# Two transformer blocks at sequence 256: other places in SBUF for the weight buffers, the 256-column activations and the chunks of the gated hidden layer

## Chip, cores and metric

The kernel runs on one core of one Trainium2 chip. The metric is the device time of one execution in microseconds. The engines are named as in the profile: PE (TensorE matmuls), PEld (its weight loads), DVE (VectorE), ACT (ScalarE), POOL (GpSimd), SP (SyncE).

## What is computed

Two transformer blocks in fp32, one after the other, on 256 positions of width 2048 (`D`). The first puts 16 meta tokens ahead (272 positions, `T`), and runs neighbourhood attention, latent attention and a gated MLP with a short convolution. The second is conditioned on a vector `c` and runs a gated convolution, a gated linear recurrence over 8 heads, two output gates and a second gated MLP. Cut to the products with large weights:

```python
# first block, h: 272 x 2048
proj = rmsnorm(h) @ w_in                          # 2048 x 3904
q, kv = rmsnorm(cq) @ w_q_up, rmsnorm(ckv) @ w_kv_up
h = h + concat(rmsnorm(out_a), rmsnorm(out_b)) @ w_out
hn = rmsnorm(h)
h = h + (silu(conv3(hn @ w_gate)) * (hn @ w_up)) @ w_down      # D_FF = 5632
# second block, x: 256 x 2048
mod = silu(c) @ w_ada + b_ada                     # scales, shifts and gates
proj = (rmsnorm(x) * (1 + sc_m) + sh_m) @ w_in_2  # 2048 x 11264
merged = sigmoid(gate_a) * (conv_part @ w_conv_out) + sigmoid(gate_b) * (hgrn_part @ w_hgrn_out)
x = x + gt_m * (merged @ w_o)
h2 = rmsnorm(x) * (1 + sc_f) + sh_f
x = x + gt_f * ((silu(h2 @ w_ffn_gate) * (h2 @ w_ffn_up)) @ w_ffn_down)
return rmsnorm(x)
```

## The kernel before

**Layout.** Activations are kept transposed: 128 features on the partitions, positions along the free axis. A chunk is 128 features by 256 (or 272, or 258) positions. `D` is 16 chunks (`KD`), half of `D_FF` is 22 (`HALF`).

**Split products.** A product in fp32 precision is made of three in fp32r. Each weight and each activation is split in a hi part and a lo part (what is left), and hi times hi, hi times lo and lo times hi are added up in PSUM. Weights come by DMA in slabs of 2048 columns of 4 bytes (`raw`, three buffers); ACT copies the hi part to `wh` (line 1301), DVE subtracts and writes the lo part to `wl` (line 1811); both have three buffers `wh0..wh2`, `wl0..wl2`, of 8192 bytes a partition each. An activation tile has a first axis of 2, hi plane and lo plane: `xx` (272 columns a chunk), `xs`, `hid`, `conv`, `oo` (256 columns a chunk).

**The gemm.** The host part lays out all products as slabs and gemms in one order (`make_plan`), and every engine's program walks the same order, tied together by semaphores. In `gemm` (lines 704 to 706) a slab of 256 output columns has 8 chunks of weights; for each chunk k and each of two column tiles j of 128 there are three matmuls:

- line 704: weights `wh`, moving operand the hi plane of chunk k
- line 705: weights `wh` again, moving operand the lo plane of chunk k
- line 706: weights `wl`, moving operand the hi plane of chunk k

So a chunk is six matmuls, and each has its own weight load. `gemm_raw` (lines 671 to 673) does the same on activations that aren't scaled yet, `gemm_by_head` (lines 732 to 734) for the latent attention. Attention, the recurrence and the conditioning vector run as generators ("lanes") that are pumped between the chunks of the gemms.

**Places.** What the change touches is the place of an operand, its byte address within a partition modulo 256 (`ROW_BYTES`). `row_home(offset, place)` gives the next address at a wanted place. `wh` starts at place 128. All slabs, chunks and column tiles of weights are multiples of 256 bytes apart, so all weights in `wh` are read from place 128. Between `wh` and `wl` lie `rstd` and two tiles `ssq`, so `wl` is at 128 + 192 = 64 (mod 256). `xx` follows `wl`, at place 64. Its chunks are 1088 bytes long, each 64 further on than the one before. A gemm that reads columns 16 to 271 (the up gemms of the first gated block, 256 columns) so reads chunk k from place 128 + 64k, one that reads columns 14 to 271 (its gate gemms, 258 columns) from 120 + 64k. `xs`, `hid`, `conv` and `oo` have chunks of 1024 bytes, and are placed at `wh_off + 64`: every chunk in both planes is read from place 192.

**The gated hidden layer.** `hid` holds 22 chunks, hi and lo. For each unit ACT writes the hi part (line 1660) and DVE the lo part (line 2257), and the eight down gemms of each half read them all: 32 down gemms in the kernel, of 22 chunks. While a gated block begins, its input (`raw_ffn`, `raw_mix`) lies in the same memory, before `hid` is written.

Of the kernel before, what the change touches and what calls it, by code (L numbers as in the profile page):

```python
# [7 lines left out]
F32 = mybir.dt.float32  # L8
# [5 lines left out]
P = 128  # L14
# [12 lines left out]
GRID = 64  # L27
SLAB = 2048
ROW_BYTES = 256

ORDER = "q0 m0 k0 v0 q1 m1 k1 v1 m2 q2 k2 v2 m3 q3 k3 v3".split()

# [273 lines left out]
def build(nc, A, out):  # L306
    ctx = ExitStack()
    with ctx:
# [9 lines left out]
        def sb(name, shape, dt=F32):  # L318
            t, cursor[0] = at(name, shape, dt, cursor[0])
            cursor[0] = (cursor[0] + 31) // 32 * 32  # L320
            return t
# [7 lines left out]
        raw = [sb(f"raw{i}", [P, SLAB]) for i in range(NR)]  # L329
        wh_off = cursor[0]  # L330
        wh = [sb(f"wh{i}", [P, SLAB], F32R) for i in range(NS)]
        rstd = sb("rstd", [P, T])
        ssq = {n: sb(f"ssq_{n}", [P, T]) for n in "ha"}
        assert (cursor[0] - wh_off) % ROW_BYTES == 192
        wl = [sb(f"wl{i}", [P, SLAB], F32R) for i in range(NS)]
        xoff = cursor[0]
        xx = sb("xx", [P, 2, KD, T], F32R)
        xs, _ = at("xs", [P, 2, KD + 1, SEQ], F32R, row_home(xoff, wh_off + 64))
        hoff = cursor[0]
        H = sb("H", [P, KD, T])  # L340
        cst = sb("cst", [P, NCONST])
# [5 lines left out]
        nx_off = cursor[0]  # L347
        nx = [sb(f"nx{i}", [P, T]) for i in range(NXB)]
        sqt = [sb(f"sqt{i}", [P, T]) for i in range(2)]
        ssq["b"] = sb("ssq_b", [P, T])  # L350
        ada_off = cursor[0]
        ada_raw = [sb(f"ada_raw{i}", [P, 512]) for i in range(NADA)]
        ada_acc = sb("ada_acc", [P, 512])
# [36 lines left out]
        assert off <= mla_end  # L390

        raw_in, _ = at("raw_in", [P, 2, KD, T], F32R, limit // 32 * 32 - 8 * KD * T)
        ffn_home = row_home(arena, wh_off + 64)
        raw_ffn = [at(f"raw_ffn{i}", [P, 2, 8, T], F32R, ffn_home + (2 + 22 * i) * SEQ * 4)[0] for i in range(2)]
        raw_mix, _ = at("raw_mix", [P, 2, 6, T - Q0], F32R, ffn_home + 2 * HALF * SEQ * 4)
        cursor[0] = ffn_home
        hid = sb("hid", [P, 2, HALF, SEQ], F32R)
        gct = [sb(f"gc{i}", [P, SEQ]) for i in range(NGC)]

        cursor[0] = mix_home = row_home(arena, wh_off + 64)  # L400
        conv = sb("conv", [P, 2, 8, SEQ], F32R)
        cursor[0] = oo_home = row_home(cursor[0], wh_off + 64)
        oo = sb("oo", [P, 2, 8, SEQ], F32R)
        cu = sb("cu", [P, 2, SEQ])
        cy = sb("cy", [P, 2, SEQ])
# [14 lines left out]
        cu2 = sb("cu2", [P, 2, SEQ])  # L420
        cy2 = sb("cy2", [P, 2, SEQ])

        OPERAND = {X0: xx, XS: xs, XQ: cqx, XKV: ckvx, XB: xb, XHID: hid, XOC: conv, XOH: oo}
        NORM_DST = [xx, cqx, ckvx, xb, xx, xx]
        NORM_T0 = [0, Q0, 0, Q0, Q0, Q0, 16, 16]
        NORM_D = [D, 512, 256, 1024, 1024, D, D, D]
# [212 lines left out]
        def tensor_program(pe):  # L639
# [40 lines left out]

            def gemm(key, ready=None):
                g = GEMMS[key]
                x = OPERAND[g.operand]
                n = g.t1 - g.t0
                for j, b in enumerate(g.banks):
                    if g.use[j] > 1:
                        pe.wait_ge(s_bank[b], g.use[j] - 1)
                for i in g.slabs:
                    _, _, k0, nk, _, ncols = SLABS[i]
                    last = i == g.slabs[-1]  # L690
                    h = wh[i % NS][:, 0:nk * ncols].rearrange("p (c n) -> p c n", c=nk)
                    l = wl[i % NS][:, 0:nk * ncols].rearrange("p (c n) -> p c n", c=nk)
                    for c in range(nk):
                        k = k0 + c
                        if c == 0:
                            pe.wait_ge(s_lo, 2 * i + 1)
                        if c == nk // 2:
                            pe.wait_ge(s_lo, 2 * i + 2)
                        if ready is not None:
                            ready(k)  # L700
                        end = last and c == nk - 1
                        for j, (o, w) in enumerate(g.tiles):
                            dst = ps[g.banks[j]][0:w, 0:n]
                            pe.matmul(dst, h[:, c, o:o + w], x[:, 0, k, g.t0:g.t1], start=(k == 0), stop=False)  # L704
                            pe.matmul(dst, h[:, c, o:o + w], x[:, 1, k, g.t0:g.t1], start=False, stop=False)  # L705
                            m = pe.matmul(dst, l[:, c, o:o + w], x[:, 0, k, g.t0:g.t1], start=False, stop=end)  # L706
                            if c == nk - 1 and j == len(g.tiles) - 1:
                                m.then_inc(s_slab, 1)
                        if c in ticks(nk):
                            lanes.pump(c == nk - 1 or c == nk // 2 - 1)  # L710
# [577 lines left out]
        def scalar_program(act):  # L1288
# [326 lines left out]
            def ffn(b):  # L1615
                gc_use = 2 * HALF * (b - 1)
                for f in range(2):
                    for g in range(HALF // 2):
                        gate, up = (b, "gate", f, g), (b, "up", f, g)
                        first_use = gc_use + HALF * f + 2 * g  # L1620

                        def silu():
                            yield
                            for j in range(2):
                                if f == 0 and g < 2:
                                    act.wait_ge(s_ft, 2 * g + j + 1)
                                else:
                                    act.wait_ge(*last_use(gate, j))
                                gc = gct[(first_use + j) % NGC]
                                act.activation(gc[:, :], gc[:, :], ACT.Silu).then_inc(s_silu, 1)  # L1630

                        gemm(gate)
                        act.wait_ge(s_slab, done(gate))
                        for j in range(2):
                            u = first_use + j
                            gc, src = gct[u % NGC], ps[j]
                            if u - gc_use >= NGC or b == 2:
                                act.wait_ge(s_hidl, u - NGC + 1)
                            n = HALF * f + 2 * g + j
                            if f == 0 and g < 2:  # L1640
                                act.wait_ge(*last_use(gate, j))
                            if b == 1:
                                if f == 0 and g < 2:
                                    src = ssq["ab"[j]]
                                act.activation(gc[:, :], src[:, 2:258], ACT.Identity, bias=V("cb", n), scale=V("cw1", n)).then_inc(s_gca, 1)
                            elif f == 0 and g < 2:
                                act.activation(gc[:, :], gc[:, :], ACT.Silu, bias=shift_of(4 * g + j)).then_inc(s_fu, 1)
                            else:
                                s, _ = last_use(gate, j)
                                act.activation(gc[:, :], src[:, 0:256], ACT.Silu).then_inc(s, 1)  # L1650
                        if b == 1:
                            lanes.start("silu", silu(), slow=True, front=True)
                        gemm(up)
                        lanes.drain("silu")
                        for j in range(2):
                            u = first_use + j
                            act.wait_ge(*last_use(up, j))
                            if f == 1 and g == 0 and j == 0:
                                act.wait_ge(s_slab, done((b, "down", 0, 7)))
                            act.activation(hid[:, 0, 2 * g + j, :], gct[u % NGC][:, :], ACT.Copy).then_inc(s_hidh, 1)  # L1660
                    for g in range(8):
                        gemm((b, "down", f, g))
                        for j in range(2):
                            if f == 1:
                                c = 2 * g + j
                                squares(N_MIX2 if b == 1 else 8, c, H[:, c, 16:T], *last_use((b, "down", 1, g), j))
                        if b == 1 and f == 1:
                            if g == 1:
                                act.wait_ge(s_gain, 2)
                                raw_shift_hi(N_MIX2)  # L1670
                            raw_his(N_MIX2, RAW_LAG[N_MIX2].get(g, []))
                        if b == 2 and f == 1 and g:
                            final_gain(2 * g - 2)
                            final_gain(2 * g - 1)
                        if f == 1 and g == 0:
                            ready_sqrt()
# [123 lines left out]
        def vector_program(dve):  # L1800
# [392 lines left out]
            def ffn(b):  # L2193
                gc_use = 2 * HALF * (b - 1)
                for f in range(2):
                    for g in range(HALF // 2):
# [37 lines left out]
                        for j in range(2):  # L2234
# [19 lines left out]
                            else:  # L2254
                                dve.tensor_tensor(gc[:, :], ps[2 + j][:, 0:256], gc[:, :], ALU.mult).then_inc(s, 1)
                            dve.wait_ge(s_hidh, u + 1)
                            dve.tensor_tensor(hid[:, 1, 2 * g + j, :], gc[:, :], hid[:, 0, 2 * g + j, :].bitcast(F32), ALU.subtract).then_inc(s_hidl, 1)
                    if b == 2 and f == 0:
                        mod_until(24)
                    for g in range(8):  # L2260
# [278 lines left out]
```

## Time and profile before

| | |
|---|---|
| median of 3 runs | 2701.86 us (2701.0 to 2703.86) |
| the profiled execution's own time | 2700.86 us |
| its span, first to last instruction | 2699.5 us |
| granted clock of TensorE, mean | 0.995 |
| PE busy | 2645.3 us, 98% |
| DVE, ACT, POOL busy | 68%, 46%, 12% |
| matmuls | 22052 |
| of them with 256 columns at a constant place (xs, hid, conv, oo, in `gemm`) | 3 x 4544 = 13632 |

Matmuls overlap, so the busy time of one (some 280 ns) is longer than the distance from its start to the start of the next. That distance is read from the timeline, as the start of one matmul subtracted from the start of a later one, divided by the number between them.

### The profile page before, as it was taken

The numbers are of one execution on the slowest core, as the hardware profiler recorded it, in microseconds if no ns is written. First come the engines' busy times: TensorE is split into PE (matmuls) and PEld (weight loads), VectorE is DVE, ScalarE is ACT, GpSimd is POOL, SyncE is SP. The second block draws the span as 40 slices with busy tenths as digits, with TensorE's granted clock in tenths as the row PEclk, the third lists the DMA queues.
The fourth block names the chain that finished last, engine by engine and source line by source line (L and its number), as shares of the span: only waits on it lengthen the run. The fifth ranks groups of instructions, "written<-read, shape, count | busy, mean of one in ns | idle before, by whom it ended". The sixth has DMA issues, their size and how long they took to land.

```text
span 2699.5 us, 51384 instructions
## 1 busy us (share of the span) xinstructions
PE 2645.3 (98%) x22052; PEld 2606.7 (97%) x22052; DVE 1844.0 (68%) x2592; ACT 1248.4 (46%) x1943; POOL 331.5 (12%) x526
## 2 busy tenths in 40 slices
PE   7999999999999999999999999999999999999998
PEld 7888889999999999999999999999999999999998
DVE  6666568877777777787888667776877644444444
ACT  5556655544433444445444443334554443444443
POOL 2110101111121111231000001110211000000001
PEclk9999999999999999999999999999999999999999
DMA  6433345678788887886444568886768656555553
GB/s 204 137 106 103 118 148 173 205 267 269 263 293 278 277 270 262 272 285 207 152 147 155 188 225 279 273 279 217 256 208 273 219 192 191 195 188 190 187 186 126
DMA packets 500084, 571.22 MB, mean 212 GB/s; under 512 B 26704, under 2 KB 473424, under 8 KB 499856
## 3 DMA queue, kind: packets, MB, share of 16 engines
q1 hardware_dynamic: 467968, 463.76, 52.6%
q0 software_dynamic: 31600, 103.80, 11.9%
q8 instruction: 174, 2.85, 0.4%
q10 hardware_dynamic: 288, 0.36, 0.1%
q14 instruction: 54, 0.44, 0.0%
HBM read 565.77 MB, written 2.54 MB: 211 GB/s over the span
## 4 chain that ended last, share of the span: by engine, by line
PE 86%; DVE 7%; ACT 4%; issue 1%; DMA 1%; POOL 0%; SPq 0%; DVEq 0%; ACTq 0%
PE ps L704 27%; PE ps L705 27%; PE ps L706 26%; DVE wl L1811 3%; ACT wh L1301 2%; PE ps L1002 1%; PE ps L833 1%; DMA raw<-in_w_in 1%; DVE nx L1915 1%; DVE lr L2007 1%; ACT lp L1476 0%; PE ps L806 0%; PE ps L858 0%; PE ps L859 0%; PE ps L671 0%
## 5 line engine op out<-in xcount | busy, mean ns | idle before, releaser
L1811 DVE TENSOR_TENSOR wl<-raw,wh 128x1024 fp32r<-128x1024 f32 (+1 forms) x894 | 1058.9, 1200 | 577.0 <-ACT wh L1301 572.7
L1301 ACT ACTIVATE wh<-raw 128x1024 fp32r<-128x1024 f32 (+1 forms) x894 | 883.2, 1030 | 606.1 <-PE ps L706 587.8
L704 PE MATMUL ps<-xs,wh 128*128 128x256 f32 x2880 | 811.3, 282 | 5.8 <-DVE xs L1892 5.8
L705 PE MATMUL ps<-xs,wh 128*128 128x256 f32 x2880 | 799.4, 278 | 0.0
L706 PE MATMUL ps<-xs,wl 128*128 128x256 f32 x2880 | 796.7, 277 | 0.0
L704 PEld LDWEIGHTS ps<-xs,wh 128*128 128x128 f32 x2880 | 539.9, 187 | 7.6 <-DVE wl L1811 5.8
L705 PEld LDWEIGHTS ps<-xs,wh 128*128 128x128 f32 x2880 | 545.0, 189 | 1.0 <-issue 1.0
L706 PEld LDWEIGHTS ps<-xs,wl 128*128 128x128 f32 x2880 | 539.5, 187 | 0.0
L704 PE MATMUL ps<-xx,wh 128*128 128x258 f32 (+3 forms) x1840 | 530.2, 288 | 3.7 <-DVE xx L1894 3.7
L705 PE MATMUL ps<-xx,wh 128*128 128x258 f32 (+3 forms) x1840 | 522.3, 284 | 0.0
L706 PE MATMUL ps<-xx,wl 128*128 128x258 f32 (+3 forms) x1840 | 522.3, 284 | 0.0
L704 PE MATMUL ps<-hid,wh 128*128 128x256 f32 x1408 | 393.4, 279 | 0.0
L705 PE MATMUL ps<-hid,wh 128*128 128x256 f32 x1408 | 390.1, 277 | 0.0
L706 PE MATMUL ps<-hid,wl 128*128 128x256 f32 x1408 | 388.8, 276 | 0.0
L704 PEld LDWEIGHTS ps<-xx,wh 128*128 128x128 f32 (+1 forms) x1840 | 347.9, 189 | 8.8 <-DVE wl L1811 3.7
L1162 POOL DMA_DIRECT2D ada_raw<-in_w_ada x384 | 206.7, 538 | 1193.4 <-DVE ada_acc L2060 1055.7
L705 PEld LDWEIGHTS ps<-xx,wh 128*128 128x128 f32 (+1 forms) x1840 | 348.3, 189 | 0.7
L706 PEld LDWEIGHTS ps<-xx,wl 128*128 128x128 f32 (+1 forms) x1840 | 347.5, 189 | 0.0
L2060 DVE SCALAR_TENSOR_TENSOR ada_acc<-ada_raw,small,ada_acc 128x512 f32<-128x512 f32 x360 | 268.4, 746 | 0.0
L705 PEld LDWEIGHTS ps<-hid,wh 128*128 128x128 f32 x1408 | 266.2, 189 | 0.0
L704 PEld LDWEIGHTS ps<-hid,wh 128*128 128x128 f32 x1408 | 263.4, 187 | 0.0
L706 PEld LDWEIGHTS ps<-hid,wl 128*128 128x128 f32 x1408 | 263.3, 187 | 0.0
(378 smaller groups left out, 2753.2 us busy)
## 6 DMA issues: line engine op xcount, KB each, us to landing
raw<-in_w_in SPq DMA_DIRECT2D x118, 1024.0 KB, 5.3
ada_raw<-in_w_ada POOLq DMA_DIRECT2D x384, 256.0 KB, 4.8
raw<-in_w_gate SPq DMA_DIRECT2D x44, 1024.0 KB, 6.5
raw<-in_w_up SPq DMA_DIRECT2D x44, 1024.0 KB, 7.1
raw<-in_w_ffn_gate SPq DMA_DIRECT2D x44, 1024.0 KB, 5.2
raw<-in_w_ffn_up SPq DMA_DIRECT2D x44, 1024.0 KB, 5.3
raw<-in_w_down SPq DMA_DIRECT2D x32, 1024.0 KB, 6.0
raw<-in_w_ffn_down SPq DMA_DIRECT2D x32, 1024.0 KB, 5.4
```

What stands on the lines that cost most here:

```text
L704: pe.matmul(dst, h[:, c, o:o + w], x[:, 0, k, g.t0:g.t1], start=(k == 0), stop=False)
L705: pe.matmul(dst, h[:, c, o:o + w], x[:, 1, k, g.t0:g.t1], start=False, stop=False)
L706: m = pe.matmul(dst, l[:, c, o:o + w], x[:, 0, k, g.t0:g.t1], start=False, stop=end)
L833: m = pe.matmul(bank[0:w, 0:keys_of(j)], l[:, o:o + w], r[:, 0:keys_of(j)], start=(i == 0), stop=(i == len(qk) - 1))
L1002: m = pe.matmul(bank[:, 128 * j:128 * j + 128], k[:, n, 128 * b:128 * b + 128], q[:, n, 128 * b:128 * b + 128], start=True, stop=True)
L1162: pool.dma_start(ada_raw[i % NADA][:, :], w[:, k, 512 * g:512 * g + 512]).then_inc(s_ada[i % NADA], 16)
L1301: act.activation(wh[i % NS][:, part], raw[i % NR][:, part], ACT.Copy).then_inc(s_hi, 1)
L1811: dve.tensor_tensor(wl[i % NS][:, part], raw[i % NR][:, part], wh[i % NS][:, part].bitcast(F32), ALU.subtract).then_inc(s_lo, 1)
L1915: dve.scalar_tensor_tensor(out=x, in0=norm_src(n, i), scalar=norm_gain(n, i), in1=rstd[:, 0:m], op0=ALU.mult, op1=ALU.mult).then_inc(s_nx, 1)
L2007: dve.reciprocal(r[:, :], r[:, :]).then_inc(s_ldve[lane], 1)
L2060: dve.scalar_tensor_tensor(out=ada_acc[:, :], in0=r, scalar=s, in1=ada_acc[:, :], op0=ALU.mult, op1=ALU.add).then_inc(s_acc, 1)
```

## The change

All weights go to place 128 (`rstd` and `ssq` move behind, to the small tiles), `xs`, `hid`, `conv` and `oo` go from place 192 to place 64, and `xx` starts at place 128 in place of 64. In `hid` the chunks are no longer all at one place: after every fourth chunk there is a gap of 8 columns (32 bytes), so chunks 0 to 3 are at place 64, 4 to 7 at 96, 8 to 11 at 128, 12 to 15 at 160, 16 to 19 at 192, 20 and 21 at 224. A plane of `hid` gets 64 columns more, so that the lo plane has the same places. The number, order, shapes and waits of all instructions stay.

```diff
+HID_STEP = 8
+HID_PLANE = HALF * 256 + 64
...
         wh = [sb(f"wh{i}", [P, SLAB], F32R) for i in range(NS)]
-        rstd = sb("rstd", [P, T])
-        ssq = {n: sb(f"ssq_{n}", [P, T]) for n in "ha"}
-        assert (cursor[0] - wh_off) % ROW_BYTES == 192
+        assert (cursor[0] - wh_off) % ROW_BYTES == 0
         wl = [sb(f"wl{i}", [P, SLAB], F32R) for i in range(NS)]
         xoff = cursor[0]
         xx = sb("xx", [P, 2, KD, T], F32R)
-        xs, _ = at("xs", [P, 2, KD + 1, SEQ], F32R, row_home(xoff, wh_off + 64))
+        xs, _ = at("xs", [P, 2, KD + 1, SEQ], F32R, row_home(xoff, wh_off - 64))
...
-        ssq["b"] = sb("ssq_b", [P, T])
+        rstd = sb("rstd", [P, T])
+        ssq = {n: sb(f"ssq_{n}", [P, T]) for n in "hab"}
...
-        ffn_home = row_home(arena, wh_off + 64)
-        raw_ffn = [at(f"raw_ffn{i}", [P, 2, 8, T], F32R, ffn_home + (2 + 22 * i) * SEQ * 4)[0] for i in range(2)]
-        raw_mix, _ = at("raw_mix", [P, 2, 6, T - Q0], F32R, ffn_home + 2 * HALF * SEQ * 4)
+        ffn_home = row_home(arena, wh_off - 64)
+        raw_ffn = [at(f"raw_ffn{i}", [P, 2, 8, T], F32R, ffn_home + (2 * SEQ + i * HID_PLANE) * 4)[0] for i in range(2)]
+        raw_mix, _ = at("raw_mix", [P, 2, 6, T - Q0], F32R, ffn_home + 2 * HID_PLANE * 4)
         cursor[0] = ffn_home
-        hid = sb("hid", [P, 2, HALF, SEQ], F32R)
+        hid = sb("hid", [P, 2, HID_PLANE], F32R)
...
-        cursor[0] = mix_home = row_home(arena, wh_off + 64)
+        cursor[0] = mix_home = row_home(arena, wh_off - 64)
         conv = sb("conv", [P, 2, 8, SEQ], F32R)
-        cursor[0] = oo_home = row_home(cursor[0], wh_off + 64)
+        cursor[0] = oo_home = row_home(cursor[0], wh_off - 64)
         oo = sb("oo", [P, 2, 8, SEQ], F32R)
...
+        def hidden_at(h, c):
+            return hid[:, h, c * SEQ + c // 4 * HID_STEP:(c + 1) * SEQ + c // 4 * HID_STEP]
+
+        def moving(g, h, k):
+            return hidden_at(h, k) if g.operand == XHID else OPERAND[g.operand][:, h, k, g.t0:g.t1]
...
-                            pe.matmul(dst, h[:, c, o:o + w], x[:, 0, k, g.t0:g.t1], start=(k == 0), stop=False)
-                            pe.matmul(dst, h[:, c, o:o + w], x[:, 1, k, g.t0:g.t1], start=False, stop=False)
-                            m = pe.matmul(dst, l[:, c, o:o + w], x[:, 0, k, g.t0:g.t1], start=False, stop=end)
+                            pe.matmul(dst, h[:, c, o:o + w], moving(g, 0, k), start=(k == 0), stop=False)
+                            pe.matmul(dst, h[:, c, o:o + w], moving(g, 1, k), start=False, stop=False)
+                            m = pe.matmul(dst, l[:, c, o:o + w], moving(g, 0, k), start=False, stop=end)
...
-                            act.activation(hid[:, 0, 2 * g + j, :], gct[u % NGC][:, :], ACT.Copy).then_inc(s_hidh, 1)
+                            act.activation(hidden_at(0, 2 * g + j), gct[u % NGC][:, :], ACT.Copy).then_inc(s_hidh, 1)
...
-                            dve.tensor_tensor(hid[:, 1, 2 * g + j, :], gc[:, :], hid[:, 0, 2 * g + j, :].bitcast(F32), ALU.subtract).then_inc(s_hidl, 1)
+                            dve.tensor_tensor(hidden_at(1, 2 * g + j), gc[:, :], hidden_at(0, 2 * g + j).bitcast(F32), ALU.subtract).then_inc(s_hidl, 1)
```

## Rows read from the trace of the kernel before

**Rows 1.** The page: busy time of each engine, and the granted clock in 40 slices.
```profile
PE 2645.3 (98%) x22052; PEld 2606.7 (97%) x22052; DVE 1844.0 (68%) x2592; ACT 1248.4 (46%) x1943; POOL 331.5 (12%) x526
...
PEclk9999999999999999999999999999999999999999
```

**Rows 2.** The waits of PE: total us, times, longest us.
```profile
PE ps L671 <- DVE wl L1811: 15.0, 2, 14.1
```

**Rows 3.** Groups by line and shape: busy us, mean ns | idle us before.
```profile
L704 PE MATMUL ps<-xs,wh 128*128 128x256 f32 x2880 | 811.3, 282 | 5.8 <-DVE xs L1892 5.8
L705 PE MATMUL ps<-xs,wh 128*128 128x256 f32 x2880 | 799.4, 278 | 0.0
L706 PE MATMUL ps<-xs,wl 128*128 128x256 f32 x2880 | 796.7, 277 | 0.0
L704 PE MATMUL ps<-hid,wh 128*128 128x256 f32 x1408 | 393.4, 279 | 0.0
L705 PE MATMUL ps<-hid,wh 128*128 128x256 f32 x1408 | 390.1, 277 | 0.0
L706 PE MATMUL ps<-hid,wl 128*128 128x256 f32 x1408 | 388.8, 276 | 0.0
...
L704 PE MATMUL ps<-xx,wh 128*128 128x256 f32 x672 | 189.1, 281 | 3.5 <-DVE xx L1894 3.5
L705 PE MATMUL ps<-xx,wh 128*128 128x256 f32 x672 | 188.7, 281 | 0.0
L706 PE MATMUL ps<-xx,wl 128*128 128x256 f32 x672 | 188.5, 281 | 0.0
...
L2257 DVE TENSOR_TENSOR hid<-gc,hid 128x256 fp32r<-128x256 f32 x88 | 37.5, 426 | 42.7 <-ACT hid L1660 42.7
...
L704 PE MATMUL ps<-conv,wh 128*128 128x256 f32 x128 | 35.8, 280 | 0.0
L704 PE MATMUL ps<-oo,wh 128*128 128x256 f32 x128 | 35.7, 279 | 0.0
```

**Rows 4.** Timeline of PE (start us, us): first chunks of gemms of hid and xs, last ones.
```profile
2243.32 0.28 PE L704 MATMUL ps<-hid,wh 128*128 128x256 f32 x1
...
2246.09 0.28 PE L704 MATMUL ps<-hid,wh 128*128 128x256 f32 x1
...
2257.88 0.28 PE L704 MATMUL ps<-hid,wh 128*128 128x256 f32 x1
...
1686.64 0.28 PE L704 MATMUL ps<-xs,wh 128*128 128x256 f32 x1
...
1691.49 0.28 PE L704 MATMUL ps<-xs,wh 128*128 128x256 f32 x1
```

**Rows 5.** Timeline of PE: starts of chunks 0, 4 to 8 and 15, an up gemm.
```profile
529.65 0.28 PE L704 MATMUL ps<-xx,wh 128*128 128x256 f32 x1
...
532.46 0.28 PE L704 MATMUL ps<-xx,wh 128*128 128x256 f32 x1
...
533.17 0.28 PE L704 MATMUL ps<-xx,wh 128*128 128x256 f32 x1
...
533.89 0.28 PE L704 MATMUL ps<-xx,wh 128*128 128x256 f32 x1
...
534.60 0.28 PE L704 MATMUL ps<-xx,wh 128*128 128x256 f32 x1
...
535.30 0.28 PE L704 MATMUL ps<-xx,wh 128*128 128x256 f32 x1
...
540.27 0.28 PE L704 MATMUL ps<-xx,wh 128*128 128x256 f32 x1
```

**Rows 6.** Timeline of PEld: the load that starts with the matmul at 2246.09.
```profile
2246.10 0.19 PEld L705 LDWEIGHTS ps<-hid,wh 128*128 128x128 f32 x1
```

**Rows 7.** Timeline of PE: starts of chunks 0 and 15, a gate gemm.
```profile
587.07 0.28 PE L704 MATMUL ps<-xx,wh 128*128 128x258 f32 x1
...
597.86 0.28 PE L704 MATMUL ps<-xx,wh 128*128 128x258 f32 x1
```

More of the change, by code:

```diff
@@ L421, in build @@
         cy2 = sb("cy2", [P, 2, SEQ])
-        OPERAND = {X0: xx, XS: xs, XQ: cqx, XKV: ckvx, XB: xb, XHID: hid, XOC: conv, XOH: oo}
+        OPERAND = {X0: xx, XS: xs, XQ: cqx, XKV: ckvx, XB: xb, XOC: conv, XOH: oo}
+        def hidden_at(h, c):
+            return hid[:, h, c * SEQ + c // 4 * HID_STEP:(c + 1) * SEQ + c // 4 * HID_STEP]
+        def moving(g, h, k):
+            return hidden_at(h, k) if g.operand == XHID else OPERAND[g.operand][:, h, k, g.t0:g.t1]
         NORM_DST = [xx, cqx, ckvx, xb, xx, xx]
@@ L682, in gemm @@
                 g = GEMMS[key]
-                x = OPERAND[g.operand]
                 n = g.t1 - g.t0
```

## Prediction

> **What bounds the kernel now.** I read the page first, then the waits of the matmul engine, then its groups by line and shape, and last the start times of single matmuls. The page [rows 1] has PE busy in 2645.3 of 2699.5 us, DVE in 68% and ACT in 46% of it, and a granted clock of 9 tenths or more in every slice (0.995 in the mean, that is the 2.4 GHz level). So the kernel is as long as its stream of 22052 matmuls. The waits confirm it: the longest entry is 15.0 us in the first gemm [rows 2], the next is 5.8 us, ahead of line 704 on xs [rows 3], and what follows is smaller still. Nothing that feeds PE is late often enough to matter, and a DVE or ACT instruction that became some per cent faster or slower would not be seen. What is left to change is the cadence, the time from the start of one matmul to the start of the next.
>
> **How long one is busy is not the cadence.** The groups [rows 3] show 277 to 282 ns for a matmul of 256 columns, but these overlap. The starts tell more. In a down gemm of the second gated block [rows 4] line 704 starts its first chunk at 2243.32 and its last at 2257.88: 21 chunks of six matmuls in 14.56 us, 693.3 ns a chunk, 115.6 ns a matmul. In a gemm of `xs` it is 7 chunks in 4.85 us, 693 ns. In an up gemm of the first block [rows 5], same columns, same weight buffers, same clock, it is 15 chunks from 529.65 to 540.27, 708 ns a chunk, 118.0 ns a matmul. The only thing that sets them apart is where the moving operand lies. `hid` and `xs` have all chunks 1024 bytes apart, so all at place 192 of 256. `xx` has chunks of 272 columns, 1088 bytes, so each lies 64 bytes further on, and its chunk k is read from place (128 + 64k) mod 256. Inside this gemm the chunks differ too [rows 5]: chunk 4 (place 128) takes 532.46 to 533.17, 0.71 us; chunk 5 (place 192) 0.72; chunk 6 (place 0) 0.71; chunk 7 (place 64) 0.70. So placement does act on the cadence, by a few ns a matmul, and two things count: whether the place stays, and which place it is. In the weight loads of that down gemm [rows 4, 6] one sees why they could be linked: the load for the next matmul starts at 2246.10, when the present matmul starts (2246.09), so each matmul's first columns are read together with the next one's weights.
>
> **Part 1, constant-place tiles other than hid.** What I follow is the difference "place of the columns minus place of the weights that are loaded meanwhile". During lines 704, 705 and 706 those weights are in wh, wl and wh. Before, with wh at 128, wl at 64 and columns at 192, the difference is 64, 128, 64. After, with both at 128 and columns at 64, it is 192, 192, 192. The trace has no steady stream at 192, so I bound it from both sides. Nearest rows: the chunks of [rows 5]. The chunk at place 192 has differences (64, 128, 64) and takes 0.72 us; the one at place 64 has (192, 0, 192) and takes 0.70, the shortest of the four; place 0 with (128, 192, 128) and place 128 with (0, 64, 0) lie between. At the rows' 10 ns that is some 17 to 20 ns in six, about 2.8 ns a matmul in favour of 192. The steady stream, though, has already shed 27 ns of the 720 that the same differences cost in `xx`, and part of that may be the same loss. I take half, 1.4 ns. It holds for xs, conv and oo: 3 x (2880 + 128 + 128) = 9408 matmuls [rows 3], so 9408 x 1.4 ns = -13 us. The fast end is the whole 2.8 ns, -26 us.
>
> The slow end comes from [rows 3]. Among the three matmuls of a unit, line 704 is the one behind which the next load goes to the same buffer and place (wh after wh), and it is busy longest: 279 ns in `hid` against 277 and 276 for 705 and 706. If the equal place of successive weights is the cause of that, after the change all three are such: 3 x 279 against 279 + 277 + 276 is 5 ns a unit, 1.7 ns a matmul, +16 us on these 9408.
>
> **Part 2, hid.** The 22 chunks of a down gemm no longer lie at one place: four at 64, four at 96, then 128, 160, 192, and two at 224. That is 4224 matmuls in 32 gemms. Three terms. (a) Steps: in [rows 5], where the place steps at every chunk, a chunk takes 708 ns against 693 without; 15 ns a step, 5 steps a gemm, 32 gemms: +2.4 us. (b) Places that are no multiple of 64 (96, 160, 224: 10 of 22 chunks). The nearest row is a gate gemm [rows 7], read from column 14, so at places 120 + 64k and with 258 columns: 15 chunks from 587.07 to 597.86, 719 ns. Two more columns at 2.4 GHz are 0.8 ns a matmul, 5 a chunk, so 6 ns a chunk are left over 708, 1 ns a matmul, on 10/22 x 4224 = 1920 matmuls: +1.9 us. (c) The differences pass over all of (64, 128, 64)'s alternatives, whose mean chunk, 708, is 12 ns shorter than the 720 at place 192; half again, 1 ns a matmul: -4.2 us. Sum 0. Bounds: if hid falls to the mixed cadence of `xx` throughout, 118.0 instead of 115.6, 4224 x 2.4 ns = +10 us; at best (c) counts whole and the others nothing, -8 us.
>
> **Part 3, xx and the other tiles of 272 columns.** Their places move on by 64 at every chunk before and after, and over four chunks each of the three loads meets all four differences in either layout. Lines 704, 705 and 706 are busy 281 ns each in the 256-column form of `xx` [rows 3], so here the move of wl has no price by line: 0. The bound is half a ns either way on the 3 x 1840 matmuls of `xx`, 3 us.
>
> **Part 4, the rest.** `rstd` and `ssq` move to another address, the hi copy (line 1660) and the low half (line 2257) write 32 bytes further on; none gains an instruction or a wait, no DMA is added, and the order on every queue stays. The cover is PE: DVE is idle a third of the time, ACT more than half [rows 1]. 0. If this cover were gone, 88 writes of 426 ns [rows 3] would be 37 us in all, and a per cent of them is nothing.
>
> **Sum.** -13 + 0 + 0 + 0 = -13 us. The profiled execution took 2700.86 us around its span of 2699.5, so 2688; the median of the runs shown is 1 us above it, 2701.86, so 2689.
>
> **A page beside it.** The rows show that matmuls with the same columns cost 115.6 or 118.0 ns by place [rows 4, 5]. The Trainium skill, TensorE: Matmul & The Clock Gate, "Step-by-step: what each phase is for", says that TensorE reads its moving operand and its next weights through two independent ports, so that a load takes nothing from a running matmul. By that rule no placement matters and the sum would be 0. The trace disagrees. The same page, "Back-to-back issue gap", has N/2.4 + 2.5 ns from start to start, 109.2 ns at 256 columns, an estimate by which placement could give back at most 6.4 ns on each of 13632 matmuls, 87 us; no row here comes near it.
>
> **The rivals.**
>
> *Slower: equal places of successive weights cost.* It is the slow end of part 1, in hid as well: 13632 x 1.7 ns = +23 us, 2724 us. For it speaks that line 704 is busiest in every constant-place tile (279, 277, 276 in hid; 282, 278, 277 in xs; 280 and 279 for line 704 in conv and oo) [rows 3]. Against it: in `xx` the same line has the same wh-after-wh and shows nothing (281, 281, 281). It decides as soon as it costs over 1.4 ns, the gain of part 1.
>
> *No change in xs: only constancy counts.* The 27 ns between the chunk at place 192 in `xx` and the steady chunk are more than all that separates the four places. If a stream at any one place settles into the same 693 ns, part 1 is 0. In hid only (a) and (b) are left, +4 us: 2706 us, at the edge of what can be told from no change. For it: xs, hid, conv and oo have one cadence at different distances between their hi and lo halves. Against it: these all have the same differences, so they can't tell.
>
> *Hid loses its steadiness.* Part 1 is 0 and hid pays the mixed cadence, +10 us: 2712. For it: the up gemms never settle, over 15 chunks [rows 5]. Against it: they step every six matmuls, hid every 24.
>
> *Placement does nothing*, by the rule of two ports: 2702. In the form that the trace allows, the differences in `xx` come from its row length, and not from where it stands towards the weights. It has little for it, as chunks 4 to 7 have one length and differ.
>
> **How the numbers follow.** Forecast 0.46; slower by equal weights 0.20; only constancy 0.16; hid loses 0.12; nothing 0.06. The forecast's own range runs from -26 - 8 + 3 (2671) to about 2698. The range for 8 in 10 goes up to 2724, where the slow case stands, and down to 2673. A measurement of this kernel tells about 0.2%, 5.4 us, from no change. The forecast case is faster but for a tenth of it, with a little from the others: faster 0.45. Half of "only constancy", all of "nothing" and that tenth: same 0.20. The rest: slower 0.35.
>
> **What would show it.** Right: in the starts of line 704, seven chunks of `xs` in 4.80 us instead of 4.85 (685 ns each), lines 704, 705 and 706 equally busy in xs, conv and oo; 21 chunks of hid in 14.5 to 14.6 us; an up gemm's 15 chunks still in 10.6 us. Slower case: busy 279 or more on all three lines and 7 chunks in 4.92 us. Only constancy: 4.85 again, though with another split over the three lines. Hid's own case: 21 chunks in about 14.8 us. The prediction is wrong in its ground if `xs` moves by more than 3 ns a matmul either way: then a steady stream has states that the stepping stream of `xx` doesn't show.

## The result and the profile after

The changed kernel takes 2716.3 us in the median (2712.4 to 2719.0, 4 runs), the kernel before 2702.1 us in the same comparison: ratio 1.0047, 95% interval 1.0032 to 1.0062. So it is slower by 0.5%, where a faster kernel, 2689 us, had been forecast. The profiled execution took 2717.0 us. The four runs lie 6.6 us apart, those of before 2.9.

The page of the kernel after, for [rows 1]:

```profile
span 2715.6 us, 51384 instructions
...
PE 2660.4 (98%) x22052; PEld 2620.8 (97%) x22052; DVE 1844.6 (68%) x2592; ACT 1248.8 (46%) x1943; POOL 330.9 (12%) x526
```

Same instructions, same clock (0.994 against 0.995); PE is busy 15.1 us longer, and the span is 16.1 us longer. The waits of PE are as before, the largest again the first slab's, 15.8 us. The whole difference is cadence. The groups by line and shape after, for [rows 3]; the edit moved lines 704 to 706 to 710 to 712:

```profile
L710 PE MATMUL ps<-xs,wh 128*128 128x256 f32 x2880 | 811.3, 282 | 5.8 <-DVE xs L1898 5.8
L711 PE MATMUL ps<-xs,wh 128*128 128x256 f32 x2880 | 804.6, 279 | 0.0
L712 PE MATMUL ps<-xs,wl 128*128 128x256 f32 x2880 | 804.5, 279 | 0.0
L710 PE MATMUL ps<-hid,wh 128*128 128x256 f32 x1408 | 396.3, 281 | 0.0
L712 PE MATMUL ps<-hid,wl 128*128 128x256 f32 x1408 | 395.3, 281 | 0.0
L711 PE MATMUL ps<-hid,wh 128*128 128x256 f32 x1408 | 394.9, 280 | 0.0
...
L712 PE MATMUL ps<-xx,wl 128*128 128x256 f32 x672 | 187.4, 279 | 0.0
```

The three lines are now nearly alike, and hid has gone from 279, 277, 276 to 281, 280, 281. (The 282 of line 710 on xs contains 68 longer matmuls, 0.39 us in the mean, most of them behind matmuls of a lane; without them it is 279, before and after.) The starts show more. The timeline of PE in the same down gemm of hid, for [rows 4], at chunks 0, 4, 8, 12, 16, 20 and 21:

```profile
2249.79 0.28 PE L710 MATMUL ps<-hid,wh 128*128 128x256 f32 x1
...
2252.62 0.28 PE L710 MATMUL ps<-hid,wh 128*128 128x256 f32 x1
...
2255.46 0.28 PE L710 MATMUL ps<-hid,wh 128*128 128x256 f32 x1
...
2258.33 0.28 PE L710 MATMUL ps<-hid,wh 128*128 128x256 f32 x1
...
2261.16 0.28 PE L710 MATMUL ps<-hid,wh 128*128 128x256 f32 x1
...
2263.99 0.28 PE L710 MATMUL ps<-hid,wh 128*128 128x256 f32 x1
...
2264.70 0.28 PE L710 MATMUL ps<-hid,wh 128*128 128x256 f32 x1
```

21 chunks in 14.91 us against 14.56: 710 ns for the six matmuls of a chunk against 693. By fours the chunks take 2.83, 2.84, 2.87, 2.83 and 2.83 us, and the dearest, 8 to 11, are those at place 128, where the weights are too. And two stretches of xs, each from chunk 0 to chunk 7 of a gemm:

```profile
1659.90 0.28 PE L710 MATMUL ps<-xs,wh 128*128 128x256 f32 x1
...
1664.66 0.28 PE L710 MATMUL ps<-xs,wh 128*128 128x256 f32 x1
...
1737.99 0.28 PE L710 MATMUL ps<-xs,wh 128*128 128x256 f32 x1
...
1742.94 0.28 PE L710 MATMUL ps<-xs,wh 128*128 128x256 f32 x1
```

The first takes 4.76 us, 680 ns a chunk; the second 4.95 us, 707 ns. Same code, same places, same clock: there are two cadences. The kernel before has two as well, which the rows shown so far don't tell: nearly all of its stream at constant places runs at 693, but one stretch of xs doesn't. Its timeline there, ahead of four transposes of a lane (L806) and behind them:

```profile
1995.22 0.28 PE L704 MATMUL ps<-xs,wh 128*128 128x256 f32 x1
...
2025.61 0.28 PE L704 MATMUL ps<-xs,wh 128*128 128x256 f32 x1
...
2027.02 0.60 PE L806 MATMUL ps<-cst,ada_acc 128*128 128x128 f32 x4
...
2028.52 0.28 PE L704 MATMUL ps<-xs,wh 128*128 128x256 f32 x1
...
2035.46 0.28 PE L704 MATMUL ps<-xs,wh 128*128 128x256 f32 x1
```

Ahead of the transposes 43 chunks take 30.39 us, 706.7 ns each; behind them ten take 6.94, 694 each. With the 7.5 us before 1989.1 that is some 40 us of the kernel before at 707.

After the change the stream holds each cadence over long stretches; in the last gate and up gemms it stays in the slow one for 240 us. The stretch view of the kernel after there (length, then PE busy and, in brackets, the number of matmuls):

```profile
2328.00:2570.00 242.00, 242.00 (x2057) 242.00 (x2056) 118.54 (x128) 99.65 (x128) 0.00 (x0) 1.00 0.58 186
```

and of the kernel before in the same gemms:

```profile
2320.00:2560.00 240.00, 240.00 (x2079) 240.00 (x2079) 118.86 (x129) 101.34 (x130) 0.00 (x0) 1.00 0.58 190
```

242 us for 2057 matmuls is 117.6 ns each, 240 for 2079 is 115.4. After the change every chunk in this stretch takes 706 or 707 ns, though DVE is busy in half of it only and ACT in two fifths. In an up gemm of the first block, 15 chunks now run from 533.16 to 543.68, 10.52 us, where [rows 5] have 10.62.

Over all matmuls that follow each other directly, from the timeline's starts: hid went from 115.6 to 118.3 ns (+11.5 us in all), xs from 115.8 to 116.1 (+2.8), the 256-column form of `xx` from 118.0 to 117.0 (-2.0), the rest by less than half a us each. That is 11.3 of 16.1 us; 4.1 of the others lie where lane matmuls and waits interrupt the stream, about 2 of them in the attention, and 0.6 ahead of the first matmul.

### The profile page after: what moved, and what is told of

Read it like the earlier page. It is cut to its first block, busy times and chain, and to the rows that moved or that the text cites. A ratio compares the mean times of both kernels' runs of the same rounds, so it can differ in the third digit from the quotient of the medians.

```text
span 2715.6 us, 51384 instructions
## 1 busy us (share of the span) xinstructions
PE 2660.4 (98%) x22052; PEld 2620.8 (97%) x22052; DVE 1844.6 (68%) x2592; ACT 1248.8 (46%) x1943; POOL 330.9 (12%) x526
## 4 chain that ended last, share of the span: by engine, by line
PE 87%; DVE 7%; ACT 4%; issue 1%; DMA 0%; POOL 0%; SPq 0%; DVEq 0%; ACTq 0%
PE ps L710 27%; PE ps L711 26%; PE ps L712 26%; DVE wl L1817 3%; ACT wh L1307 1%; PE ps L1008 1%; PE ps L839 1%; PE ps L678 1%; PE ps L680 1%; PE ps L679 1%; DVE nx L1921 1%; DVE lr L2013 1%; DMA raw<-in_w_in 0%; PE ps L855 0%; PE ps L865 0%
## 5 line engine op out<-in xcount | busy, mean ns | idle before, releaser
L712 PE MATMUL ps<-hid,wl 128*128 128x256 f32 x1408 | 395.3, 281 | 0.0
```

Source lines behind the costliest of these rows:

```text
L712: m = pe.matmul(dst, l[:, c, o:o + w], moving(g, 0, k), start=False, stop=end)
```

## The experiments

The two theories as I held them after this profile: **(T)** what counts is the difference "place of the columns minus place of the weights loaded meanwhile"; a stream at a constant place falls into a cadence of its own for each set of differences, sometimes one of two. **(E)** Equal places of successive weights cost, the slower rival of the prediction. Below, "(a, b)" is the difference, modulo 256, when the weights loaded meanwhile are of wh, then when they are of wl: before is (64, 128), after is (192, 192). "Chunk" is the six matmuls of a chunk at a constant place, between interruptions; its ns come from the one execution that was traced. Each ratio is to the kernel before as timed together with that run.

### e1, e2: the steps in hid, taken out and put in alone

```diff
# e1, on the changed kernel
-HID_STEP = 8
-HID_PLANE = HALF * 256 + 64
+HID_STEP = 0
+HID_PLANE = HALF * 256
```
```diff
# e2, on the kernel before: hid alone as in the changed kernel
-        hid = sb("hid", [P, 2, HALF, SEQ], F32R)
+        hid = sb("hid", [P, 2, HID_PLANE], F32R)
...
+            return hid[:, h, c * SEQ + c // 4 * HID_STEP:(c + 1) * SEQ + c // 4 * HID_STEP]
```

> The changed kernel without the steps in hid: all 22 chunks at place 64. My theory from the profile after: with weights at 128 and columns at 64 a steady stream has two cadences, 680 ns and 707 ns for six matmuls, and keeps the one it is in; the steps hold hid in the slow one or above (710 ns). Then the down gemms fall from 710 ns a chunk to 680 or 707 each, chunk after chunk the same, and the kernel takes 2695 to 2714 us by how much falls into which. Rival: the steps are harmless and hid is slow because of where the gated block's tiles now lie; then hid stays at 710 and the kernel at 2716.

> The kernel before with the steps in hid alone (weights at 128 and 64, columns at 192, then 224, 0, 32, 64, 96). Theory: the steps cost by themselves, hid goes from 693 to 705-712 ns a chunk, +9 to +13 us, 2711 to 2715 us, and xs, conv and oo stay at 693. Rival: the steps cost only together with equal places of the weights; then the time stays within 2 us of 2702.

e1: 2709.3 us, ratio 1.0032 (1.0019 to 1.0045). Chunks of hid take 680 or 707 ns, 701.8 in the mean, in xs 696.6. e2: 2709.2 us, ratio 1.0026 (1.0014 to 1.0038); chunks of hid 704.9 ns in the mean, all others 693. So the steps cost about 7 us in either layout, and half of the change's loss is theirs: taken out, 2716.3 becomes 2709.3; put in, 2701.6 becomes 2709.2. e1 came out by T. e2 took its side against the rival of 2702 us, but with 704.9 ns and 2709.2 us it fell just short of the 705 to 712 ns and 2711 to 2715 us expected. The size checks: hid has 704 chunks (32 x 22), and e2's 11.5 ns more on each is 8.1 us. What is left in e1, 0.3%, is the mixture of 680 and 707.

### e3, e4: one half of the placement each

```diff
# e3, on e1: weights together, columns back at 192      (64, 64)
-        ffn_home = row_home(arena, wh_off - 64)
+        ffn_home = row_home(arena, wh_off + 64)
...
# e4, on the kernel before: only the columns move to 64   (192, 0)
-        ffn_home = row_home(arena, wh_off + 64)
+        ffn_home = row_home(arena, wh_off - 64)
...
```

The other three homes (xs, conv, oo) are moved in the same way, here and in the sweep below.

> All weights at 128 as after, columns at 192 as before, no steps: the difference is 64 for all three matmuls. Theory of two states: a steady stream has its own cadences at each difference, so the 693 of before goes and something else comes, in one or two values that are held over whole gemms; whether below or above I can't say. Rival, equal places of successive weights cost: all three matmuls of a unit are as line 704 was before, 118.3 ns, so six take 710 ns, +23 us, 2725 us. Rival, only constancy counts: 693 ns and 2702 us.

> The kernel before with only the columns moved from place 192 to 64; weights stay at 128 and 64, so the differences are 192, 0, 192 for the three matmuls. In the stepping stream of xx the chunk with these differences took 704 ns before. Theory of the difference: other than 693, near 700-707, +5 to +15 us (2707 to 2717). Rival, only equal weights matter: the stream keeps 693 ns and one state, 2702 us.

e3: 2728.4 us, ratio 1.0101 (1.0086 to 1.0116), chunks at 707 ns but for three short stretches of xs at 680, the longest 7.5 us. e4: 2729.8 us, 1.0108 (1.0093 to 1.0124), also 707, but for one stretch of xs of 33 us. Two starts in it, six matmuls apart:

```profile
2010.80 0.28 PE L704 MATMUL ps<-xs,wh 128*128 128x256 f32 x1
...
2011.53 0.28 PE L704 MATMUL ps<-xs,wh 128*128 128x256 f32 x1
```

That is 0.73 us; over the whole stretch it is 733 ns a chunk. So T's two states are there at (64, 64) and at (192, 0) too, with one of them rare. T's times for e4, 2707 to 2717 us, were 13 us short: 13.3 ns on each of 2272 chunks (13632 / 6) is 30 us, not 5 to 15. Each half alone is worse than the whole change, by 19 and 20 us against e1; the change can't be taken apart into a good and a bad half. E's 710 ns and 2725 us for e3 look nearly right. But E is wrong as the cause: e4 keeps the weights apart and is as slow as e3, and e1 with the weights together is faster than both. "Only constancy counts", 2702 us for both, fell as well.

### e5 to e8: the difference swept, weights together, no steps

```diff
# on e1: columns at 0 (e5), 128 (e6), 32 (e7), 96 (e8)
-        ffn_home = row_home(arena, wh_off - 64)
+        ffn_home = row_home(arena, wh_off + 128)        # e6: + 0, e7: + 160, e8: + 224
...
```

> As the changed kernel without steps, but columns at place 0 (weights at 128, difference 128 for all three matmuls). So far: difference 64 gives only 707 ns for six matmuls, 192 gives 680 or 707. In the kernel before, line 705 with difference 128 came second (115.9 ns). Theory, every difference has its own set of states: 680, 693 or 707 throughout or mixed, 2671 to 2727 us; I lean to a share of 680, since two differences apart from 128 both know 707 and the mixed triple of before had 693. Rival, 707 is what equal weights give and 680 is special to 192: 707 throughout, 2727 us.

> Columns at place 128, same as the weights (difference 0). If two reads of the same place at the same time collide, this is the worst of the sweep, above 707 ns for six matmuls, over 2728 us. If the difference only shifts the phase of the stream: 680 to 707 ns, 2671 to 2727 us.

> Columns at place 32 (difference 160), half a 64-byte line off. Theory, the cadence goes by lines of 64 bytes: a column run that straddles lines costs, at or above 707 ns for six matmuls, 2727 us or more. Rival, it is between its neighbours 128 and 192.

> Columns at place 96 (difference 224), half a line off on the other side of 192. Same expectation as for 160: at or above 707 ns by the theory of 64-byte lines; by the rival near 192's mixture of 680 and 707, 2709 us.

| | difference | chunk, ns | time, us | ratio to before |
|---|---|---|---|---|
| e6 | 0 | 720 | 2758.9 | 1.0206 (1.0176 to 1.0235) |
| e3 | 64 | 707, a little 680 | 2728.4 | 1.0101 (1.0086 to 1.0116) |
| e5 | 128 | 708 to 715 | 2741.1 | 1.014 (1.011 to 1.0169) |
| e7 | 160 | 701 to 715 | 2735.3 | 1.0118 (1.0089 to 1.0148) |
| e1 | 192 | 680 or 707 | 2709.3 | 1.0032 (1.0019 to 1.0045) |
| e8 | 224 | 706 to 715 | 2736.3 | 1.0122 (1.0093 to 1.0151) |

e5 to e8 have two executions each, at most 3.7 us apart. The timeline of PE in e6, first and last chunk of the same down gemm:

```profile
2285.43 0.28 PE L710 MATMUL ps<-hid,wh 128*128 128x256 f32 x1
...
2300.55 0.28 PE L710 MATMUL ps<-hid,wh 128*128 128x256 f32 x1
```

15.12 us for 21 chunks, 720 ns each, and hid, conv and oo keep 720 in the whole kernel (a few chunks of xs take 712 to 715). My lean for e5 was wrong: 128 has no 680. 192 is the best of the six. e7 and e8 are above 707, as the theory of 64-byte lines had it, but their means, 709.5 and 710, also lie between those of their neighbours (712 at 128, 699 at 192 with its two states together, 720 at 0), so whether straddling a line costs stays open. And the map explains hid after the change: its chunks at places 64, 96, 128, 192 stand at differences 192, 224, 0 and 64, and took mostly 707, 707 to 712, 713 to 720 and 707 to 712. Those at 160 and 224, differences 32 and 96 that I haven't swept in a steady stream, took 707 to 712 and 710 to 716.

### e9 to e12: a pair of different differences

```diff
# e9, on e1: wl 64 bytes further than wh                   (192, 128)
-        assert (cursor[0] - wh_off) % ROW_BYTES == 0
+        cursor[0] += 64
# e10, on e1: wl 128 bytes further (place 0)              (192, 64)
-        assert (cursor[0] - wh_off) % ROW_BYTES == 0
+        mod = sb("mod", [P, 96])
+        assert (cursor[0] - wh_off) % ROW_BYTES == 128
...
-        mod = sb("mod", [P, 96])
# e11, as e10 but columns at wh_off + 64                   (64, 192)
# e12, on the kernel before: columns at wh_off + 128       (128, 192)
```

> The two weight buffers at different places: wh at 128, wl at 192, columns at 64, no steps in hid. Differences 192 with wh and 128 with wl. Measured so far for six matmuls: (192, 192) 680 or 707, (192, 0) 707, (64, 64) 707, (128, 128) 712, (64, 128) 693. Theory A, the pair matters and wl at another place takes away one of the two states of 192: 680 throughout would be 2672 us, 707 throughout 2729. Theory B, the cadence of a unit is the mean of what each difference gives alone: (2 x 693 + 712)/3 = 700 ns, 2714 us. B already fails for the kernel before (709 expected, 693 measured).

> wh at 128, wl at 0, columns at 64, no steps: differences 192 and 64. A: one of the states 680, 693, 707, held throughout (2672, 2702 or 2729 us). B: (2 x 693 + 707)/3 = 698 ns, 2711 us.

> wh at 128, wl at 0, columns at 192, no steps: differences 64 and 192. A: one of 680, 693, 707, held throughout. B: (2 x 707 + 693)/3 = 702 ns, 2719 us.

> The kernel before with the columns moved from place 192 to 0: differences 128 and 192, weights still 64 apart. In the stepping stream of xx before, the chunk at place 0 had these and took 711 ns. A: a state of its own, 680 to 713. B: (2 x 712 + 693)/3 = 706 ns, 2727 us.

| | pair | chunk, ns | time, us | ratio to before |
|---|---|---|---|---|
| e9 | (192, 128) | 705 to 714 | 2735.7 | 1.0111 (1.0082 to 1.0141) |
| e10 | (192, 64) | 680 | 2677.5 | 0.9896 (0.9867 to 0.9925) |
| e11 | (64, 192) | 680 or 713 | 2707.6 | 1.0012 (1.0001 to 1.0023) |
| e12 | (128, 192) | 707, in places 703 to 723 by turns | 2734.3 | 1.0106 (1.0077 to 1.0135) |

e9, e10 and e12 have two executions each, e11 nine. e10 is faster than both kernels. B, the mean of single differences, fails in three of four: it had 700, 698 and 702 ns for e9, e10 and e11. For e12 it had 706 ns and 2727 us, which the measured 707 can't refute. A, one state held throughout, holds in e10 and nearly in e12; e9 has several values in turn, from 705 to 714, and e11 two states, like the change. Eight of the nine executions of e11 took 2701.6 to 2707.7 us and one, the profiled one, 2737.4. In its trace all of hid and most of xs is at 713; that the other eight spent more of their time at 680 is likely, but they have no trace. `xx` lies behind wl and moves with it; its chunks take 707 to 709 ns in all four.

The timeline of PE in e10, first and last chunk of the down gemm, 14.28 us for 21 chunks:

```profile
2227.50 0.28 PE L710 MATMUL ps<-hid,wh 128*128 128x256 f32 x1
...
2241.78 0.28 PE L710 MATMUL ps<-hid,wh 128*128 128x256 f32 x1
```

How it keeps one state where the change has two is seen at an interruption. In both, four transposes of a lane (L812) break the stream now and then. The kernel after, before and after such a break:

```profile
1697.30 0.28 PE L710 MATMUL ps<-xs,wh 128*128 128x256 f32 x1
...
1697.64 0.28 PE L710 MATMUL ps<-xs,wh 128*128 128x256 f32 x1
...
1697.98 0.60 PE L812 MATMUL ps<-cst,ada_acc 128*128 128x128 f32 x4
1698.34 0.36 PE L710 MATMUL ps<-xs,wh 128*128 128x256 f32 x1
...
1698.77 0.28 PE L710 MATMUL ps<-xs,wh 128*128 128x256 f32 x1
...
1699.13 0.28 PE L710 MATMUL ps<-xs,wh 128*128 128x256 f32 x1
```

Ahead of it three matmuls take 0.34 us (680 ns for six); behind it 0.36 (707 for six), and from there the stream stays at 707 for 67 chunks, 47 us, until the next transposes. e10 at such a break, one line 710 in two:

```profile
2014.56 0.28 PE L710 MATMUL ps<-xs,wh 128*128 128x256 f32 x1
...
2015.24 0.60 PE L812 MATMUL ps<-cst,ada_acc 128*128 128x128 f32 x4
2015.59 0.37 PE L710 MATMUL ps<-xs,wh 128*128 128x256 f32 x1
...
2016.39 0.28 PE L710 MATMUL ps<-xs,wh 128*128 128x256 f32 x1
...
2017.09 0.28 PE L710 MATMUL ps<-xs,wh 128*128 128x256 f32 x1
...
2017.77 0.28 PE L710 MATMUL ps<-xs,wh 128*128 128x256 f32 x1
```

The chunk that begins at 2016.39 takes 0.70 us, the next 0.68 again: it is thrown out too, and comes back. So it does behind every interruption in the traces of e10, e13 and e15, within two chunks. Why this pair comes back and the others don't isn't shown.

### e13 to e15: the winner again, with steps, and moved as a whole

```diff
# e14, on e10: the steps of the change in hid
-HID_STEP = 0
-HID_PLANE = HALF * 256
+HID_STEP = 8
+HID_PLANE = HALF * 256 + 64
# e15, on e10: everything 64 bytes further on
+        cursor[0] += 64
         raw = [sb(f"raw{i}", [P, SLAB]) for i in range(NR)]
```

> The kernel with wh at 128, wl at 0, columns at 64 again (differences 192 and 64), timed with more rounds: 2675 to 2680 us, ratio 0.988 to 0.992, if the stream comes back to 680 ns for six matmuls after every interruption. Were 680 only one of two states that it was caught in, as with (192, 192) and (64, 192), some executions would lie 10 to 50 us higher.

> The same with the steps of the changed kernel in hid (32 bytes after every fourth chunk). The theory that a step is a change of the difference: chunks 0 to 3 stay at 680 ns, the others take what other differences give, 700 to 720, hid 708 to 712 in the mean, 704 x 29 ns = +20 us, 2697 us. Rival, steps cost a fixed amount by themselves, the +7 us that they cost in the other two layouts: 2684 us.

> All of it moved on by 64 bytes: wh at 192, wl at 64, columns at 128; the differences stay 192 and 64. If only differences count: 680 ns throughout and 2677 us. If the absolute places count: another cadence, 693 to 720 ns, 2700 us or more.

e13: 2676.0 us (2673.6 to 2676.7), ratio 0.99 (0.9885 to 0.9914): 680 is found again in the trace, and with the two of e10 all six executions of this kernel lie between 2673.6 and 2678.5. e14: 2696.0 us, 0.9975 (0.9965 to 0.9984), 20 us above e13. Its down gemm by the timeline of PE, at chunks 0, 1, 4 and 8:

```profile
2239.06 0.28 PE L710 MATMUL ps<-hid,wh 128*128 128x256 f32 x1
...
2239.76 0.28 PE L710 MATMUL ps<-hid,wh 128*128 128x256 f32 x1
...
2241.80 0.28 PE L710 MATMUL ps<-hid,wh 128*128 128x256 f32 x1
...
2244.64 0.28 PE L710 MATMUL ps<-hid,wh 128*128 128x256 f32 x1
```

Chunks 1 to 3, still at place 64, take 2.04 us, 680 ns each; chunks 4 to 7, one step on, 2.84, 710 each. Over the kernel a chunk of hid takes 708.8 ns in place of 680.2, and 704 x 28.6 ns is the 20 us measured. So a step has no fixed price: it costs what the next difference costs. e15: 2675.7 us, 0.9899 (0.9883 to 0.9916), 680 ns: with every tile 64 bytes further on nothing changes, so the absolute places don't matter, the differences do.

## Why the prediction was wrong

**Part 1, xs, conv and oo, -13 us** is the step that failed. It extrapolated a cadence from a stream that steps to one that doesn't: "The steady stream, though, has already shed 27 ns of the 720 ... I take half". The order was right, 192 is the best single difference (e1, e3, e5, e6). But a steady stream doesn't have a cadence near a mean, it has states (at some differences a few values in turn, as in e9). With (192, 192) it has two, 680 and 707 ns, on either side of the 693 that (64, 128) keeps nearly everywhere. 680 throughout would have been worth -21 us on these 9408 matmuls, near the fast end; the mixture gave +2.4 (+2.8 in xs, -0.4 in conv and oo). The last line of the prediction named this as its way to be wrong in its ground, but put it as a move of more than 3 ns a matmul; the states are only 2.2 ns off 693 either way. The sign of the slower case, busy 279 or more on all three lines and 7 chunks in 4.92 us, was there in part: 281, 280, 281 in hid, 4.95 us in one gemm of xs, 4.76 in the other.

The input of part 1 was thin as well. It read one up gemm, where the chunk at place 192 takes 0.72 us and the one at 64 takes 0.70. In another up gemm of the same trace the chunk at place 192 starts and ends so:

```profile
506.61 0.28 PE L704 MATMUL ps<-xx,wh 128*128 128x256 f32 x1
...
507.30 0.28 PE L704 MATMUL ps<-xx,wh 128*128 128x256 f32 x1
```

That is 0.69 us. Over all 21 up gemms, 15 of the 84 chunks at place 192 take 694 ns, most of the others 719; their mean is 710.4, against 704.5 at place 64. That is 1 ns a matmul in favour of 192 and not 2.8, and nothing was "shed" for good. So the stepping stream, too, had two values for one place, and the steady stream of xs had its 40 us at 707: the states stood in the trace of the kernel before.

**Part 2, hid, 0 us**, was wrong in size and by part 1's rule: measured +11.5 us, just beyond the bound of +10 (the rival "hid loses its steadiness", 2712 us, is nearest to what happened, though not by its mechanism). Term (a), a fixed price for each step, is not what happens (e14); the first chunk behind a step is somewhat off the next ones, 712 against 707 at chunks 12 and 16 after the change, 707 against 714 at chunk 4 in e14. Term (c) credited the other differences with a gain; in a steady stream nearly all of them are above 693 (e3 to e8), and hid's chunks 0 to 3, at difference 192, mostly took 707, the longer of their two cadences.

**Part 3, xx, 0 us**: -2.0 us in its 256-column form; its place of wl does have a price after all, 708 ns a chunk with wl apart and 701.6 with the weights together (e1, e3, e5 to e8). It is within the bound of 3.

**Part 4** holds in its waits: none of PE has changed by more than 1 us. But no term had the 4.1 us between and behind the matmuls of the lanes, and what makes them isn't traced further.

**The rivals.** Slower by equal weights: e4 refutes it, since it is as slow with the weights apart. Only constancy: refuted by e6. Placement does nothing, the rule of two independent ports (the Trainium skill, TensorE: Matmul & The Clock Gate, "Step-by-step: what each phase is for"): refuted by the 81 us between e6 and e10, which differ in nothing but places. That it is a conflict between the two reads is argued from the difference being what counts (e15), not shown: the trace has no counter for it. A rival to it, collisions with what ACT, DVE and the DMA read and write meanwhile, is at odds with the evenness: these come and go, while chunks stay at 706 or 707 over 240 us after the change and at 720 in e6.

Whether the place counts modulo 256 or 512 can be told from the layout: in the kernel before and in e10, xs lies an odd multiple of 256 bytes from hid, conv and oo, and all four have the same main cadence, 693 and 680. So the period is no longer than 256 bytes as far as these layouts tell, and differences 0, 64, 128 and 192 differ, so it isn't 64 or 128.

## What to carry to other kernels

All of this is shown for fp32r matmuls of 256 columns, each with a weight load of its own. When TensorE is the bound and its matmuls follow each other without a break, measure the distance from start to start per stretch and over the whole trace, not the busy time and not in one gemm. If it depends on the address modulo 256, what counted here is the place of the moving operand minus the place of the weights loaded meanwhile, and a stream of one set of differences can have more than one cadence that it keeps. Sweep the whole set together on the chip (a pair of differences isn't the sum of its parts), look at how the stream comes out of its interruptions, and prefer a set that returns to its shortest cadence over one that only has it. For the choice here that meant weights at 128 and 0 and columns at 64, 1% below the kernel before; a tile that drifts through the places loses it (hid in e14, xx in all layouts).

## What the hardware showed that I had not expected

- Five cadences for six matmuls of 256 columns at the 2.4 GHz level, 680, 693.3, 706.7, 720 and 733.3 ns (the last in e4 alone), all 13.3 ns apart, 32 periods of that clock. Some differences give others between (705, 709, 711, 713 to 715).
- Two cadences for one and the same stretch of code, kept over 67 chunks, 47 us, and over 240 us in the last gate and up gemms. Five of the pairs of differences have two: (64, 128), (192, 192), (64, 64), (192, 0), (64, 192). What picks one of the two after an interruption stays open: after the change the same four transposes left the stream slow at 1698 us and fast at 1651 us. I have not tried to steer it.
- The same kernel can differ by 1% from run to run at the same granted clock: 2701.6 to 2707.7 us in eight executions of e11, 2737.4 in the ninth. The two states are the likely reason; only the ninth has a trace.
- The lowest cadence seen, 113.3 ns a matmul, was found at (192, 192), (64, 64), (192, 64) and (64, 192); no placement here came lower. The formula of the Trainium skill for an isolated matmul (TensorE: Matmul & The Clock Gate, "Back-to-back issue gap"), N/2.4 + 2.5 ns, gives an estimate of 109.2 for 256 columns, which no run here shows.
